# TensorE's first expert stands in front of the loop, with the weighted down biases inside its body

## The reference, cut to what matters

```python
g = xb @ w_gate[e] + b_gate[e]
u = xb @ w_up[e] + b_up[e]
g = jnp.minimum(g, SWIGLU_LIMIT)
u = jnp.clip(u, -SWIGLU_LIMIT, SWIGLU_LIMIT)
act = g * jax.nn.sigmoid(SWIGLU_ALPHA * g) * (u + 1.0)
return act @ w_down[e] + b_down[e]
...
y = jnp.zeros((n_tok + 1, d), jnp.float32).at[row_tok].add(yb * row_w[:, None])
```

## Time and profile before

| what | us |
|---|---|
| median of 3 runs | 2179.81 |
| the three runs | 2176.15 to 2181.65 |
| profiled execution, its own time | 2181.77 |
| its span, first to last instruction | 2180.0 |
| experts, TensorE, first L1493 to end of last combine | 327.8 to 1288.3 |

### The profile page before, as it was taken

How to read it: one execution, slowest core, us unless ns; L and a number is a source line. 1 busy time by engine, 2 the same in 40 slices (tenths; PEclk the granted TensorE clock), 3 DMA queues, 4 the chain that set the end, 5 groups by cost and what they waited for, 6 DMA issues and landing times.

```text
span 2180.0 us, 24259 instructions
## 1 busy us (share of the span) xinstructions
PE 1917.8 (88%) x9685; PEld 1052.8 (48%) x9686; DVE 592.1 (27%) x1167; ACT 404.8 (19%) x584; POOL 60.8 (3%) x82
## 2 busy tenths in 40 slices
PE   5989997899999887889888679988999899979997
PEld 4744452233333222223222238547884577758863
DVE  4657241221212111212121122421000279620001
ACT  2230122211222121112211131111000244210000
POOL 2000010000000000000000010003001000000000
PEclk9999998999999899999999889989999999999999
DMA  9644758998899999998999992073440323064420
GB/s 316 217 175 175 260 200 358 428 427 359 365 428 428 428 428 428 428 427 318 428 428 427 428 397 91 20 272 116 155 155 22 122 93 126 22 256 149 149 71 20
DMA packets 106224, 574.45 MB, mean 264 GB/s; under 512 B 7271, under 2 KB 8803, under 8 KB 81552
## 3 DMA queue, kind: packets, MB, share of 16 engines
q1 hardware_dynamic: 102000, 563.46, 64.8%
q0 software_dynamic: 4160, 10.06, 1.6%
HBM read 572.42 MB, written 1.07 MB: 263 GB/s over the span
## 4 chain that ended last, share of the span: by engine, by line
PE 73%; DMA 14%; DVE 6%; ACT 4%; issue 2%; SPq 1%; DVEq 0%; ACTq 0%
PE ps L1976 14%; DMA ring<-in_w_up 12%; PE ps L1459 11%; PE ps L1987 7%; PE ps L709 5%; PE ps L1500 5%; PE ps L1473 4%; PE ps L1521 3%; PE ps L895 2%; PE ps L1483 2%; PE ps L717 2%; PE ps L2463 1%; PE ps L1020 1%; DMA ring<-in_w_in 1%; PE ps L1433 1%
## 5 line engine op out<-in xcount | busy, mean ns | idle before, releaser
L1976 PE MATMUL ps<-arena,ring 128*128 128x256 f32 x1408 | 304.4, 379 | 1.8 <-issue 1.8
L1976 PEld LDWEIGHTS ps<-arena,ring 128*128 128x128 f32 x1408 | 267.4, 190 | 38.4 <-issue 2.1
L1459 PE MATMUL ps<-ring,arena 128*64 128x512 f32 x1088 | 240.5, 595 | 0.0
L1500 PE MATMUL ps<-ring,arena 128*32 128x512 f32 x1088 | 146.1, 685 | 61.6 <-DMA ring<-in_w_up 61.6
L1987 PE MATMUL ps<-ring,arena 128*128 128x512 f32 x352 | 151.4, 592 | 0.0
L1459 PEld LDWEIGHTS ps<-ring,arena 128*64 128x64 f32 x1088 | 75.3, 137 | 152.4 <-issue 152.1
L709 PE MATMUL ps<-arena,ring 128*128 128x256 f32 x608 | 132.8, 380 | 0.0
L1473 PE MATMUL ps<-ring,arena 128*64 128x512 f32 x544 | 120.5, 594 | 12.5 <-ACT arena L1422 12.5
L709 PEld LDWEIGHTS ps<-arena,ring 128*128 128x128 f32 x608 | 115.0, 190 | 16.8 <-issue 1.5
L1500 PEld LDWEIGHTS ps<-ring,arena 128*32 128x32 f32 x1088 | 35.3, 124 | 159.6 <-issue 88.0
L1987 PEld LDWEIGHTS ps<-ring,arena 128*128 128x128 f32 x352 | 66.9, 190 | 83.3 <-issue 83.2
(11 more groups left out here) (592 smaller groups left out, 2027.2 us busy)
## 6 DMA issues: line engine op xcount, KB each, us to landing
ring<-in_w_gate SPq DMA_DIRECT2D x64, 2048.0 KB, 18.9
ring<-in_w_up SPq DMA_DIRECT2D x64, 2048.0 KB, 21.6
ring<-in_w_down SPq DMA_DIRECT2D x64, 2048.0 KB, 19.3
ring<-in_ffn_w_gate_up SPq DMA_DIRECT2D x22, 2048.0 KB, 8.2
ring<-in_ada_w SPq DMA_DIRECT2D x12, 2048.0 KB, 11.6
ring<-in_ffn_w_down SPq DMA_DIRECT2D x10, 2048.0 KB, 7.8
ring<-in_w_in SPq DMA_DIRECT2D x8, 2048.0 KB, 21.0
ring<-in_dn_w_in SPq DMA_DIRECT2D x6, 2048.0 KB, 7.8
```

The costliest lines, as they stand in the source:

```text
L1459: m = pe.matmul(bank(b)[c * CAP:(c + 1) * CAP, :], xT[:, j * P + h * CAP:j * P + (h + 1) * CAP], w[h][:, j, c * 512:(c + 1) * 512], start= ...
L1500: m = pe.matmul(bank(0)[(2 * i + c) * FEW:(2 * i + c + 1) * FEW, :], XT[:, j * P + h * CAP:j * P + h * CAP + FEW], w[h][:, j, c * 512:(c + ...
L1976: m = pe.matmul(bank(b0 + g)[:, c * SEQ:(c + 1) * SEQ], w[:, k, (2 * g + c) * P:(2 * g + c + 1) * P], hT2[:, k, :], start=(k == 0), stop=( ...
```

## The change

TensorE alone takes expert 0 in front of its loop, with its own copy of `few`, `narrow` and the out-of-line bodies; its loop starts at expert 1. VectorE, ScalarE and SP keep theirs. `pe_down_bias` leaves `pe_weights_turned` and is called (`opened`) in expert 0's copies, in `few` and `narrow` behind the gate and up products, in the large case at the top. In the copy for expert 0 the expert's number is a constant.

```diff
             pe.wait_ge(bias_in, 16 * 5)
-            pe_down_bias(pe)
...
-        def pe_few(pe, e, there):
+        def pe_few(pe, e, there, opened):
...
                 if h == 0:
                     pe_weights(pe, main, n)
+            if opened is not None:
+                opened()
             pe_gather(pe, main, n + 1)
...
-            with eng.Fori(0, E) as e:
-                n_e = eng.value_load(cnt[0:1, bass.ds(e, 1)], min_val=0, max_val=SEQ)
+
+            def expert(e, which, opened):
+                n_e = eng.value_load(cnt[0:1, e:e + 1] if isinstance(e, int) else cnt[0:1, bass.ds(e, 1)], min_val=0, max_val=SEQ)
...
+                        if opened is not None:
+                            opened()
+                        eng.br_cond(n_e > 2 * CAP, f"more_{which}", f"pair_{which}")
...
+            larges = []
+            if opened is not None:
+                larges.append(expert(0, which + "_0", opened))
+            with eng.Fori(0 if opened is None else 1, E) as e:
+                larges.append(expert(e, which, None))
+
+            def behind():
+                for large in larges:
+                    large()
+            return behind
...
+                                 opened=lambda: pe_down_bias(pe))
```

More of the change, by code:

```diff
@@ L1550, in dve_few, with pe_narrow @@
             dve.tensor_tensor(act_[0:CAP, :], um[0:CAP, :], sg[0:CAP, :], ALU.mult).then_inc(main.a_ready, 1)
-        def pe_narrow(pe, e, there):
+        def pe_narrow(pe, e, there, opened):
             n = e + 1
@@ L1699, in dve_further, with expert_rounds @@
             dve_glu(dve, extra, x, (extra.g_ps, x), (extra.u_ps, x), (0, 1), actf)
-        def expert_rounds(eng, few, narrow, wide, further, first=None):
+        def expert_rounds(eng, few, narrow, wide, further, first=None, opened=None):
             which = eng.engine.name
@@ L1713, in expert_rounds @@
                 nc.switch_bb(f"few_{which}", parent=fork)
-                few(e)
+                few(e, opened)
                 eng.br(f"next_{which}")
@@ L1718, in expert_rounds @@
                 nc.switch_bb(f"small_{which}", parent=fork)
-                narrow(e)
+                narrow(e, opened)
                 eng.br(f"next_{which}")
                 nc.switch_bb(f"next_{which}", parent=fork)
[L1723 to L1734, removed]
-                        eng.reg_add(rounds, rounds, 1)
-                        further(e, r, eng.snap(rounds))
-                    eng.br(f"pair_{which}")
-                nc.switch_bb(f"done_{which}", parent=tail)
@@ L1739, in expert_rounds, with large @@
-            return large
+                def large():
+                    eng.br(f"done_{which}")
+                    tail = nc.cur_bb
+                    with nc.body(f"large_{which}", parent=fork, valid_engines=[eng.engine]):
+                        trunk = nc.cur_bb
+                        if opened is not None:
+                            opened()
+                        eng.br_cond(n_e > 2 * CAP, f"more_{which}", f"pair_{which}")
+                        nc.switch_bb(f"pair_{which}", parent=trunk)
+                        eng.reg_add(rounds, rounds, 1)
+                        wide(e, eng.snap(rounds))
+                        eng.br(f"next_{which}")
+                        nc.switch_bb(f"more_{which}", parent=trunk)
+                        for r in range(2, ROUNDS):
+                            eng.reg_add(rounds, rounds, 1)
+                            further(e, r, eng.snap(rounds))
+                        eng.br(f"pair_{which}")
+                    nc.switch_bb(f"done_{which}", parent=tail)
@@ L1741, in pe_s7 @@
+                return large
+            larges = []
+            if opened is not None:
+                larges.append(expert(0, which + "_0", opened))
[5 more added lines that the diff above has]
+            return behind
         def pe_s7(pe):
@@ L1751, in pe_s7 @@
             pe_weights_turned(pe)
-            return expert_rounds(pe, lambda e: pe_few(pe, e, there(e)), lambda e: pe_narrow(pe, e, there(e)),
-                                 lambda e, x: pe_wide(pe, e, x, there(e)), lambda e, r, x: pe_further(pe, e, x, there(e)))
+            return expert_rounds(pe, lambda e, opened: pe_few(pe, e, there(e), opened), lambda e, opened: pe_narrow(pe, e, there(e), opened),
+                                 lambda e, x: pe_wide(pe, e, x, there(e)), lambda e, r, x: pe_further(pe, e, x, there(e)),
+                                 opened=lambda: pe_down_bias(pe))
         def dve_s7(dve):
-            return expert_rounds(dve, lambda e: dve_few(dve, e), lambda e: dve_narrow(dve, e), lambda e, x: dve_wide(dve, e, x),
+            return expert_rounds(dve, lambda e, opened: dve_few(dve, e), lambda e, opened: dve_narrow(dve, e), lambda e, x: dve_wide(dve, e, x),
                                  lambda e, r, x: dve_further(dve, e, r, x), lambda e: dve_bias_of(dve, e))
@@ L1762, in act_s7 @@
             act_weights_turned(act, o)
-            return expert_rounds(act, lambda e: act_few(act, e), lambda e: act_narrow(act, e), lambda e, x: act_wide(act, e, x),
+            return expert_rounds(act, lambda e, opened: act_few(act, e), lambda e, opened: act_narrow(act, e), lambda e, x: act_wide(act, e, x),
                                  lambda e, r, x: act_further(act, x))
```

## The result

| kernel | median, us | runs |
|---|---|---|
| before | 2176.75 | 5, 2176.15 to 2181.65 |
| changed | 2200.39 | 5, 2191.57 to 2206.51 |

Ratio 1.0095, 95% interval 1.0077 to 1.0114: slower, as forecast, but by 23.6 us from median to median where the likeliest case said 10. A second set of the changed kernel gave 1.0065 (1.0043 to 1.0087). By these ratios the two sets give 21 and 14 us, and that is the size to explain.

The account below looks back on a forecast made before the run. TensorE's 7.16 us bias product delays the loads; then TensorE and loads alternate, and experts 3 to 5 and the wide ones are TensorE's. +2 from (a) to (d) and +8.2 from (e) gave +10: median 2190, range 2181 to 2204.

Parts of the forecast that it names:

- likeliest case: Stalls behind expert 1 and on entering the first wide expert: +10 us, median 2190, chance 0.50.
- (a): Start of expert 0 without the bias product: opening 5.8 us earlier, expert 1's first load 4.5 earlier (2.9 to 5.8).
- (b): Bias product behind expert 0's second half: 3.6 us, 6.2 us to L1440, 3.0 more; expert 0 ends 1.5 earlier.
- (c): End of expert 0: the jump to `next` stalls 6.1 us as before, no loss or gain.
- (d): End of expert 1: a new 6.1 us stall at the jump to `next`; expert 3 starts 2 us later.
- (e): Entering expert 6, the first wide one: 6.2 us stall plus 2 of half clock, 8.2 us (5 to 9.5).
- third rival: Wide body pushes out loop code: two to five more 6.1 us stalls on returns or second entry; 2202 to 2220, chance 0.18.
- the first case: The likeliest case: stalls behind expert 1 and on entering the first wide expert, 2190 us, chance 0.50.

Follow-up runs that it names:

- fourth kernel: The swapped kernel with expert 0's `narrow` also placed behind everything, so its `few` runs straight into the loop's head; 2174.26 us, ratio 0.9973.
- the last one: The fourth kernel with the bias product one step further back in expert 0, behind the gather; 2174.45 us, ratio 0.9974.
- the swapped kernel: The changed kernel with the loop's large case right behind the loop's end and expert 0's never-run one behind it; 2180.17 us, ratio 0.9997.
- padded kernels: The kernel before with never-run rounds for over 128 tokens in front of `wide` on TensorE: 1,040 instructions, 2194.54 us; 522 instructions, 2193.39 us.
- the kernel with a span of 1,573: The kernel before with 522 never-run instructions moved from behind `wide` to in front of it on TensorE; 2193.39 us, ratio 1.0048.
- fifth kernel: The kernel before with the bias product done twice in front of expert 0; 2184.53 us, ratio 1.0028.
- the sixth: The kernel before with TensorE's `narrow` moved behind the loop's end, ahead of `wide`; 2180.98 us, ratio 1.0003.
- seventh kernel: The fourth kernel with the loop's `narrow` also placed behind the loop's end; 2179.64 us, ratio 1.0002.
- third kernel: The changed kernel with the bias product back in front of expert 0, expert 0 still ahead of the loop; 2196.25 us, ratio 1.0073.

## Why the prediction was right, and where it was short

The direction, the mechanism of the gain and that of the first stall at the wide expert were right, and the time fell inside the range; the likeliest case was too low, as it left out a second stall. That the sum of the first profile, 13.4 us, lies near the forecast 10 is in part luck: the stall forecast behind expert 1 did not come, and one that was not forecast came instead. By its steps:

(a) The start: 5.8 us forecast, 6.0 measured. Expert 1's first load: 4.5 forecast, 7.5 measured, outside my 5.8. I had the clock low until 327.6 because it was low at that place before. In the first profile of the changed kernel it was full from the start (L1499 3.57 us for its first half, above); in the second it was half for the first few us, and the load went out 6.0 us earlier, near my best case:

```profile
320.61 2.05 PE ps L1492 x2
322.66 4.06 PE ps L1499 x32
326.72 0.37 PE ps L1445 x2
327.09 3.57 PE ps L1499 x32
330.66 3.91 PE ps L1289 x8
```

So the clock at this place differs between executions, and in both the half-clock stretch was shorter than I forecast. My figure is among those that occur: in the profiles of the fourth kernel and of the last one, where the instructions up to this load are the same, the first half ran at half clock for longer (5.4 and 5.7 us), and the load went out 4.7 and 4.4 us earlier than before. What sets its length I cannot tell; I took the one reading of before for a fixed one.

(b) The product took 3.63 us (3.91 in the second profile), as forecast. L1439 came 7.85 us behind the end of the up product, not 6.2, as the gather behind it ran at half clock (3.48 us).

(c) The stall behind expert 0: 5.3 us of idle for 6.1 forecast. That it stayed as before was right; that it was free before is shown (0.1 us at expert 3 without it). With the loads out earlier it was no longer free: without it the swapped kernel gained 5.9 us more.

(d) The stall behind expert 1: absent in the first profile, 6.8 us of idle in the second. I took one value for something that varies. The four profiles of swapped kernels with `narrow` of the loop in its old place had it every time (5.6 to 6.1 us of idle), so the pattern was right for these. With the unused code behind the loop it was there in one profile of three (the changed kernel's second; not its first, and not that with the bias product in front).

(e) Entering the first wide expert: 8.2 us forecast, 8.4 measured.

The step that fell short is the sentence behind (e), "The second wide expert finds its code there, as does every later turn". The return from the first wide expert stalled too, in code that 6 experts had run: 7.3 us in the first profile (4.4 of idle, 2.9 of half clock), and the branch is as long in the second (6.02 us). That was in my third rival, at 0.18 and two to five stalls; one came. So the truth lies between the first case and the third. The padded kernels show that the rival's worth was more than I gave: they stalled on the second entry instead. Sum by the first profile: experts -5.2 at the start of expert 3 (81.9 for 87.1), +8.4 and +7.3 for the wide one, and +2.9 over the rest of the stage, which I have not split further: +13.4. By the second profile +2.0 at expert 3, my own figure, and +18.2 at the end.

The rule of the Trainium skill that I weighed ("Runtime: NRT & Kernel Launch", section "Instruction fetch mechanics": a taken branch whose target is outside the two-page window has to fetch; a page is 16 KiB or 256 instructions) names the kind of stall seen here, without a price. These runs do not fit its window. The branch out of `few` goes over 264 instructions and can stay within two pages, so it does not decide; the loop's way back, over some 530 instructions, more than the 512 of two pages, does. It was short in every turn, here in the changed kernel:

```profile
L1749 PEldq COMPARE_BRANCH  x31: 76/208/237, 382.6 to 1307.4; - x31
```

Nor do the runs fit a plain room of 2,048 instructions, the size that the same section gives for TensorE, as the kernel with a span of 1,573 stalled on a second entry.

What stays open is which code is held and which goes. Every layout with unused code between the loop and `wide` had two or three stalls at expert 6 or expert 21 (the second wide one), but not the same ones: first entry and first return (changed kernel, twice), both entries (both padded kernels), both entries and the second return (bias in front). In the eight profiles without unused code there (the kernel before and seven of the experiments) neither wide expert had one. Each edit also shifts the code against the 16 KB blocks in which it is fetched, and that was not varied by itself: in the fifth kernel, where a few more instructions stand in front of an unchanged loop, the branch behind expert 0 took 0.42 us and not 6.4, and whether that is the shift or the difference between executions is not shown. How the instruction memory chooses I could not see.

## What to carry to other kernels

Peeling a turn off a loop copies its rarely used branches as well; put the copies that never run at the very end, and leave directly behind the loop what the loop does jump to. Compare the sequencer's branch times (minimum against maximum) before and after: a branch of 0.2 us that takes 6 once, in a stretch where TensorE is the limit, costs that and the half clock that follows. A product in front of a stage can cost about its own time in the end if the loads of the next turn hang on what follows it: 7.2 us of product against 6.6 us of gain in one layout here, 3.7 us of added product against 6.1 us of loss (3.5 to 8.9), and next to nothing between the sixth and the seventh kernel.

## What the runs showed of the hardware

- A branch of TensorE that stalled took 5.8 to 7.1 us, with 4.4 to 6.8 us of idle, in all kernels; one took 2.0 us (1.3 of idle). The others took 0.07 to 0.26 us, and a few at a first visit or a return 0.29 to 0.42.
- The jump to the next stage over never-run code took 6.1 to 6.5 us in eleven profiles, and 0.17 us in the two where its target stands directly behind `wide`, although `wide` had ended some 280 us earlier.
- Two more far jumps in a loop turn (out to `narrow` and back) cost 0.2 to 0.3 us with the code at hand.
- The bias product (32 rows by 512 columns) took 1072 ns a matmul in front of the experts, at half clock, and 601 ns behind the up product. The 8 matmuls of the gather behind it took 3.48 and 3.26 us in the two profiles of the changed kernel, and 1.94 us in the fourth kernel's. The product in front ran mostly at full clock in one profile (4.49 us for all of it, third kernel).
